# Four feed-forward tiles formed plainly in place of two in a one-core decoder layer, the first pair's preparation spread over their outputs

## What is computed

```python
h = layer_norm(ALPHA * x + mix @ lw['w_o'], lw['ln1_w'], lw['ln1_b'])
ff_gate, ff_up = jnp.split(h @ lw['w_ffn_in'], 2, axis=-1)
y = layer_norm(ALPHA * h + (jax.nn.silu(ff_gate) * ff_up) @ lw['w_ffn_out'], lw['ln2_w'], lw['ln2_b'])
```

## Time and profile before

| | |
|---|---|
| median of 3 runs | 1096.52 us |
| lowest and highest | 1095.71, 1101.23 us |
| the profiled execution's own time | 1098.11 us |
| its span in the trace | 1096.3 us |
| instructions | 20865 |
| TensorE (PE) busy | 1037.9 us, 95% |
| VectorE (DVE) busy | 699.0 us, 64% |
| ScalarE (ACT) busy | 453.1 us, 41% |
| mean granted TensorE clock | 0.983 of full speed |

### The profile page before, as it was taken

The page is one execution under the profiler, slowest core; times in us unless marked ns, Lnnn a source line. Parts: engine busy times, 40 slices in busy tenths (PEclk is TensorE's granted clock), DMA queues, the critical chain, the costliest instruction groups (busy, mean ns, idle before and its releaser), DMA issues.

```text
span 1096.3 us, 20865 instructions
## 1 busy us (share of the span) xinstructions
PE 1037.9 (95%) x8476; PEld 998.6 (91%) x8476; DVE 699.0 (64%) x1146; ACT 453.1 (41%) x860; POOL 163.4 (15%) x242
## 2 busy tenths in 40 slices
PE   5799999998998999999999998889999999999994
PEld 5799888996998998889999998889999999999994
DVE  3832366435587879855664766988887877622446
ACT  3533345543146555415322245555554544411221
POOL 3413000001117544540000111000000000000004
PEclk9899899999999999999999999999999999999997
DMA  8347122125332221242322446023232423332432
GB/s 263 96 127 236 39 59 58 39 58 174 120 93 59 60 78 41 88 135 78 93 81 78 122 119 164 1 74 100 84 111 77 116 78 102 101 87 78 135 103 90
DMA packets 167454, 106.73 MB, mean 97 GB/s; under 512 B 12072, under 2 KB 161248, under 8 KB 167344
## 3 DMA queue, kind: packets, MB, share of 16 engines
q1 hardware_dynamic: 161584, 85.01, 27.4%
q0 software_dynamic: 5120, 18.03, 5.2%
q10 hardware_dynamic: 656, 2.36, 0.6%
HBM read 99.42 MB, written 6.95 MB: 97 GB/s over the span
## 4 chain that ended last, share of the span: by engine, by line
PE 77%; DVE 13%; ACT 4%; issue 3%; DMA 1%; POOL 1%; SPq 1%; DVEq 0%; ACTq 0%; POOLq 0%
PE bank L847 13%; PE bank L848 12%; PE bank L849 12%; PE bank L938 7%; PE bank L941 7%; PE bank L940 7%; PE bank L895 3%; PE bank L893 3%; PE bank L894 3%; DMA w_raw<-in_w_mem_kv 1%; PE bank L1083 1%; DVE decay_q L2099 1%; ACT w_hi L1483 1%; ACT probs L1531 1%; PE bank L1247 1%
## 5 line engine op out<-in xcount | busy, mean ns | idle before, releaser
L847 PE MATMUL bank<-x_lo,w_hi 128*128 128x288 f32 x864 | 265.9, 308 | 2.0 <-DVE x_lo L2006 1.9
L848 PE MATMUL bank<-x_hi,w_lo 128*128 128x288 f32 x864 | 255.9, 296 | 0.0
L849 PE MATMUL bank<-x_hi,w_hi 128*128 128x288 f32 x864 | 255.8, 296 | 0.0
L847 PEld LDWEIGHTS bank<-x_lo,w_hi 128*128 128x128 f32 x864 | 164.2, 190 | 9.3 <-issue 6.7
L848 PEld LDWEIGHTS bank<-x_hi,w_lo 128*128 128x128 f32 x864 | 164.0, 190 | 0.1
L849 PEld LDWEIGHTS bank<-x_hi,w_hi 128*128 128x128 f32 x864 | 163.4, 189 | 0.0
L762 DVE TENSOR_TENSOR w_lo<-w_raw,w_hi 128x1024 fp32r<-128x1024 f32 x82 | 104.1, 1274 | 69.0 <-ACT w_hi L1483 68.6
L1483 ACT ACTIVATE w_hi<-w_raw 128x1024 fp32r<-128x1024 f32 x88 | 92.4, 1056 | 57.9 <-PE bank L849 37.1
L938 PE MATMUL bank<-x_sum_lo,pair_hi 128*128 128x288 f32 x320 | 95.0, 297 | 6.3 <-DVE hidden L1885 2.6
L941 PE MATMUL bank<-x_sum_hi,pair_hi 128*128 128x288 f32 x320 | 94.7, 296 | 0.0
L762 DVE TENSOR_TENSOR w_lo_out<-w_raw_out,w_hi_out 128x1024 fp32r<-128x1024 f32 (+1 forms) x30 | 35.3, 1178 | 70.4 <-ACT w_hi_out L1483 70.1
(11 more groups left out here) (328 smaller groups left out, 2548.4 us busy)
## 6 DMA issues: line engine op xcount, KB each, us to landing
w_raw<-in_w_in SPq DMA_DIRECT2D x46, 512.0 KB, 3.9
up_weights<-in_w_ffn_in SPq DMA_DIRECT2D x20, 512.0 KB, 4.0
gate_weights<-in_w_ffn_in SPq DMA_DIRECT2D x20, 512.0 KB, 5.1
w_raw_out<-in_w_ffn_out SPq DMA_DIRECT2D x20, 512.0 KB, 3.9
w_raw<-in_w_o SPq DMA_DIRECT2D x14, 512.0 KB, 3.9
w_raw<-in_w_mem_kv SPq DMA_DIRECT2D x8, 512.0 KB, 5.2
mem_ring<-in_mem_k_s POOLq DMA_DIRECT2D x8, 512.0 KB, 5.6
mem_ring<-in_mem_v_s POOLq DMA_DIRECT2D x8, 512.0 KB, 4.5
```

Of the source, the lines that this page charges most:

```text
L847: pe.matmul(bank[:, 0:n], wh, lo, start=(i == 0), stop=False)
L848: pe.matmul(bank[:, 0:n], wl, hi, start=False, stop=False)
L849: mm = pe.matmul(bank[:, 0:n], wh, hi, start=False, stop=(i == len(parts) - 1))
```

## The change

Four tiles (0 to 3) are formed plainly and 18 pairs remain. The plain outputs of tiles 2 and 3 come in the order gate half 0, gate half 1, up half 0, up half 1. The preparation of pair 0 is placed anew: token sums 0 to 2 stand one output later than before, S1, S3 and S2 two outputs later, the rest behind single outputs of tiles 1 to 3. A gate buffer is now used twice by plain tiles, hence the added wait in `wait_gate_free`.

```diff
--- before.py
+++ after.py
@@ -113,17 +113,19 @@
     if j == 0:
         return [("fg", 0, 0), ("fu", 0, 0), ("fg", 1, 0), ("fg", 0, 1), ("fu", 0, 1), ("fg", 1, 1)]
-    return [("fu", 1, 0), ("fu", 1, 1)]
...
-FIRST_PAIR = 2
+    if j == 1:
+        return [("fu", 1, 0), ("fu", 1, 1)]
+    return [(kind, j, half) for kind in ("fg", "fu") for half in range(2)]
...
+FIRST_PAIR = 4
 PAIRS = FT_ - FIRST_PAIR
 KH = KT // 2
 
@@ -385,18 +387,19 @@
     late = [out(first[1], late="all")]
     steps += [("var", 1, 1), ("norm", 1, 1)]
     late.append(out(first[2], late="all"))
-    steps += [("x_sums", 0), ("combine", "S1", 0), ("combine", "S3", 0)]
     out(first[3])
-    steps += late[0]
-    steps += [("x_sums", 1), ("combine", "S2", 0), ("pair_hi", "S1", 0)]
+    steps += late[0] + [("x_sums", 0)]
     out(first[4])
-    steps += late[1]
-    steps += [("combine", "S4", 0), ("pair_hi", "A0", 0), ("x_sums", 2)]
+    steps += late[1] + [("x_sums", 1), ("combine", "S1", 0), ("combine", "S3", 0)]
     out(first[5])
-    steps += [("pair_hi", "S24", 0), ("pair_lo", "S1", 0), ("pair_lo", "A0", 0)]
-    for key in ffn_order(1):
-        out(key)
-    steps += [("x_sums", 3), ("pair_lo", "S24", 0), ("pair_hi", "A1", 0), ("pair_lo", "A1", 0)]
+    steps += [("combine", "S2", 0), ("pair_hi", "S1", 0), ("x_sums", 2)]
+    prepare = [[("combine", "S4", 0), ("pair_hi", "A0", 0)], [("x_sums", 3), ("pair_hi", "S24", 0)],
+              [("pair_lo", "S1", 0)], [("pair_lo", "A0", 0)], [("pair_lo", "S24", 0)], [("pair_hi", "A1", 0)],
+              [("pair_lo", "A1", 0)], [], [], []]
+    for j in range(1, FIRST_PAIR):
+        for key in ffn_order(j):
+            out(key)
+            steps += prepare.pop(0)
     steps += pair_steps()
@@ -1467,6 +1470,8 @@
                 if kind == "fg":
+                    if idx >= 2:
+                        out_saved(act, ("fu", idx - 2, half))
                     return
@@ -1658,7 +1663,7 @@
                 if q == 0:
-                    out_saved(act, ("fu", 1, 1))
+                    out_saved(act, ("fu", FIRST_PAIR - 1, 1))
                 copy(dst[:], src[:, 0:TH]).then_inc(snapped, 1)
```

## The result

The changed kernel takes 1107.58 us (median of 5 runs, 1106.12 to 1108.76), the kernel before, beside it on the same chip, 1096.65 (5 runs, 1095.71 to 1101.23). The ratio is 1.009, with a 95% interval of 1.0072 to 1.0107: slower by 10.9 us, where 10.7 were forecast (1107.2, range 1103 to 1113).

A forecast was written before the change was run, and what follows sets the result against it. TensorE and its waits bound the kernel, the start of the pairs costing 8.4 us. Net +9.7 and +1.0 at y make 10.7 slower: 1108.8 against the profiled 1098.11, put at 1107.2 as median, range 1103 to 1113.

The forecast's parts named there:

- The order of SP's queue: SP's loads: pair 0's weights stand behind the added plain load that waits for up(1, 1), finished at 703.2.
- The landing: Pair 0's loads: up weights land 5.8 us after the last plain load's issue, gate weights 7.6, in turn.
- The first pause: Ahead of gate(2, 0): TensorE idles 8.9 us for a bank while VectorE waits for pair 0's weights.
- The lower clock after it: In gate(2, 0): 3.2 us at a pitch of 0.24, a loss of 1.4, free because the next output waits anyway.
- The three smaller pauses: Waits for banks ahead of gate(2, 1), up(2, 1) and pair 0: 1.5, 1.8 and 0.9 us.
- Pair 0: Start of the pairs: low parts all ready, start at 743.3, first P4 at 758.0, 32.0 later than before.
- The net term of +9.7: Up to the pairs: first P4 32.0 us later, less 22.3 for two pairs fewer.
- The y term: First y output: TensorE waits 0.7 for hidden tile 2, then 0.3 for tile 3; +1.0 us.
- The sum: Whole kernel: 9.7 + 1.0 = 10.7 us slower.
- The rival that the clock falls again: Behind the second and third pause: each costs 1.4 us at the lower clock, time 1110.0; chance 13%.
- The covered case: At gate(2, 0): no pause, pair 0's weights landed in time, 3.2 us faster, 1093.3; chance 5%.

The follow-up runs named there:

- e1: The change, but SP issues the five first loads of pair weights ahead of the four added plain loads; 1098.02 us.
- e2: The change, but hidden tiles 2 and 3 are split before the last pair ends, not at the start of the first y output; 1106.29 us.
- e3: The change with pair loads ahead of the added plain loads and pair 0's preparation dealt evenly over the outputs by a table; 1093.75 us.
- e5: The change, but the five first pair loads stand behind three of the four added plain loads, one tile's wait earlier; 1101.78 us.
- e6: Two plain tiles and 20 pairs as before the change, with separate steps for sums, high and low parts in a dealing of its own; 1095.67 us.
- e7: The change's loads, behind all added plain loads, with the even dealing of e3; 1108.33 us.
- e10: The same kernel as e7, run again beside e9 on one chip; 1104.83 us.
- e9: The changed kernel itself, run again beside e10 on one chip; 1109.56 us.
- e8: Three plain tiles, pair loads ahead, a dealing of its own, and y's third and fourth hidden tiles split before the pairs end; 1089.98 us.

## Why the prediction was right

To compare positions, 0.9 us are taken off the forecast ones, since the trace after reaches gate(0, 1) that much earlier than before (683.79 and 684.73).

- **The order of SP's queue.** Right: pair 0's loads forecast at 702.3, issued at 702.72.
- **The landing.** Right: S1 forecast 5.8 and S3 7.6 us after the last plain load's issue; they begin at 708.09 and 709.89, 5.8 and 7.6 after 702.31. The up weights landed first, in turn. The Trainium skill, DMA: Bandwidth & Descriptors (Queues, rings and completion order), says that completion is not first in, first out for one issuer, which leaves room for another order; no run here shows one.
- **The first pause.** Forecast 8.9, measured 8.88 as the forecast counts it (8.72 idle in the profile), by the chain that was named: S1, S3, gate step, bank. TensorE goes on at 711.0, forecast 711.0. e1 shows that it is the loads: it goes as a whole.
- **The lower clock after it.** Forecast 3.2 us at 0.24, a loss of 1.4; it was 4.5 us (711.0 to 715.5), a loss of 2.1. It changed nothing in the sum, for the next output waited for VectorE anyway.
- **The three smaller pauses.** Forecast 1.5, 1.8 and 0.9, measured 0.76, 1.72 and 0.75 as the forecast counts (0.60, 1.56 and 0.59 idle). The first is the mis-sized one: gate(2, 0) ended 0.7 later than forecast, at the lower clock, and so ate half of the pause; the bank came free when forecast (717.1, forecast 717.2).
- **A slip in the second of them.** The terms that the prediction prints from 718.1 on add up to 727.0, not to its 726.3; taken as printed they would have put the forecast 0.7 higher, at 11.4. The trace has 8.2 us from one bank to the next, as the 726.3 has. The printed terms are recorded durations, and a step begins before the recorded end of the one ahead: S3 is recorded with 0.69, and the gate step begins 0.61 behind it. That the written total came out is not owed to the written terms.
- **Pair 0.** Right: no wait for low parts, start at 742.0 (forecast 742.4), first P4 at 756.61 (forecast 757.1). The net term of +9.7 measured 9.3.
- **The y term.** Forecast 1.0 as pauses of 0.7 and 0.3. The profile marks one pause, of 0.62, but the starts of the matmuls show both: where 0.13 is usual, 0.91 us lie ahead of the third hidden tile and 0.29 ahead of the fourth, so 0.78 and 0.16 are lost. Behind the first P4 it is 1.2 in all, and it goes with the earlier splits of e2; where the other 0.2 or so lies was not found.

```profile
944.86 0.29 PE L898 MATMUL bank<-hidden_hi,w_hi_out 128*128 128x288 f32 x1
945.77 0.40 PE L896 MATMUL bank<-hidden_lo,w_hi_out 128*128 128x288 f32 x1 [0.62 <-DVE hidden_lo L2247]
...
946.15 0.29 PE L898 MATMUL bank<-hidden_hi,w_hi_out 128*128 128x288 f32 x1
946.44 0.40 PE L896 MATMUL bank<-hidden_lo,w_hi_out 128*128 128x288 f32 x1
```

- **The sum.** 10.7 forecast; 10.4 between the traces; 10.9 between the medians. The mechanism was right; that the size is so close is in part luck, as the slip shows, and medians of one kernel lay up to 3.5 apart here.

The rival that the clock falls again fell: behind the pauses of 0.60 and 1.56, from 716 to 942, it stands at 1.00. The rule cited for it, the Trainium skill, TensorE: Matmul & The Clock Gate (What's actually happening), that recent activity decides, might have let close pauses add up; in this trace they did not.

The covered case was priced wrong. It was to give 1093.3 once the weights are in time. e1 met that condition and took 1098.0, because a second hold-up stood behind the first; my sum had removed the first pause and taken the later ones with it. Only early loads and another dealing together, in e3, reached 1093.75.

## What to carry to other kernels

When a change puts more transfers into a queue that is issued in program order, find what the last of them waits for, and put every transfer with free buffers and a later need ahead of it; here that was 9 us of the 11. Price the removal of a wait by walking the next chain on the same engine, not by taking the whole loss away. And cover costs its own length: a plain tile costs 1.7 us more than a pair, so three tiles, evenly filled, beat both two and four (each with a dealing of its own).

## What was not expected

- **The slow matmuls behind a pause hardly grow with it.** From TensorE's new start to the end of the last pitch of 0.24 us it was 4.0 us after a pause of 2.6 (before), 4.2 after 2.56 (e1), 3.0 after 3.37 (e5), 3.8 after 4.80 (e6), 4.2 after 8.90 (e2), 4.5 after 8.72 (the change), 4.5 after 8.82 (e7), 4.7 after 8.79 (e10) and 5.0 after 8.75 (e9). None followed the pauses of 0.42 (e9) to 1.56. The stretch of lower clock itself does grow: it was 3.4 us before (706.35 to 709.8), where the first matmuls behind the pause still ran at full pitch, which is why the prediction counted 3.2, and 10.2 us in the change (705.35 to 715.6), but more than half of that lay within the pause, where it slows nothing:

```profile
706.00:711.00 5.00, 0.00 (x0) 0.00 (x0) 1.80 (x4) 0.63 (x1) 0.00 (x0) 0.50 1.16 290
```

- **The start varies more than most of these edits do.** Gate(0, 1) is reached at 681.19 in e6 and at 687.65 in e5, though no edit acts before it. The three latest, e5, e7 and e8 (686.7 to 687.7), have one thing that no other kernel here has, a stretch of lower clock between 56 and 62 us; their 400th matmul begins at 75.7 to 76.8, that of the others at 72.5 to 75.1. This is e5; in the other nine the clock of that stretch is 1.00:

```profile
56.00:59.00 3.00, 2.40 (x13) 2.43 (x13) 2.93 (x7) 1.26 (x3) 1.16 (x2) 0.72 0.82 211
```

Where the rest of the difference comes from, and why the clock falls there in some executions, stays open.
